# Inverse levels of the first mixer over all 16 heads, with the state chain of one token half between the levels of the other

## Chip, cores and metric

One core of one Trainium2 chip. The metric is the device time of one execution in microseconds (us), as the median of several runs. TensorE is called PE, VectorE DVE, ScalarE ACT, and the queue that issues all loads SP.

## What is computed

The reference runs two blocks over 256 tokens of width 2048, all in float32. The change is in the first mixer of the first block, an RWKV-7 recurrence over 16 heads of 64 channels. With a state S (64x64 per head) the reference steps token by token:

```
def step(state, inp):
    r_t, w_t, k_t, v_t, kk_t, a_t = inp
    sa = einsum('bhvk,bhk->bhv', state, -kk_t)
    state = state * w_t[:, :, None, :] + sa[..., None] * (kk_t * a_t)[:, :, None, :] + v_t[..., None] * k_t[:, :, None, :]
    return state, einsum('bhvk,bhk->bhv', state, r_t)
```

After it come a group norm over each head's 64 channels, a bonus term, a gate, and the product with `ev_w_out`. The other mixer, the feed-forward parts, the second layer and the whole second block are not touched.

## The kernel before

**The chunked form.** The kernel doesn't step over tokens. It cuts the 256 tokens into two halves of 128 (`tt` on PE and ACT, `th` on DVE) and these into four chunks `c` of 64. For every token half the work has these stages:

1. *Tokens* (`kbt`): 16 transposes bring the key-side operands BM and KM into token order (BTOK, KTOK).
2. *Pairs* (`g`): per head the products of BM and of KM (stationary, 64 rows x 128 columns) with AR (moving, 64 x 256: the "a" part and the "r" part side by side), lines 852 and 853. DVE multiplies each result by a causal mask into BF (one 128x256 tile per head) and KF.
3. *Values* (`gv`): KF times the value tokens, in two forms that alternate head by head: line 859 (stationary 128x128, moving 64 columns; result GVB) and line 860 (stationary 128x64, moving 128 columns; result YT). DVE copies both out.
4. *Inverse*: the inverse of (I - strictly lower triangular BF) by doubling, six levels `lv`. In a level DVE cuts a block pattern out of BF (TM, one mask operation per group of 4 heads); PE makes `u` = TM x M (line 875, 4 matmuls per group); ACT copies it to UU (line 1489); PE makes `m`, the updates of M and of its transpose (lines 886 and 887, 8 matmuls per group in two banks; in level 5 line 893, 4 matmuls in one bank); DVE adds them into MN (two operations per group). Level 0 has no `m`: DVE makes MN of `u` and of TM.
5. *State chain*, chunk after chunk: `x` (line 908, with the state ST), `sa` (line 918, the inverse applied; ACT copies it to SAQ, line 1498), `z` (927) and `y` (933) for the output, `s` (942, 943) for the new state, which DVE adds and scales (decay). `x` of the next chunk waits for that state.

When all is done, `group_norm_mean`, `group_norm_var` and eight DVE steps (`group_norm_step`: four reciprocals, four elementwise operations) of the token half follow. Those of half 0 are put between the work of half 1, those of half 1 stand alone at the end, before the product `ev_out` (lines 607, 612, 616).

**The order of the work.** Every engine runs a list written out by hand. All PSUM results of the mixer are "jobs": `mixer_jobs()` (line 109) gives each a number `j`; job `j` uses bank `j % 5`, PE opens it once job `j-5` is freed (`open_job`), and signals `mb_done` in the order of the numbers. Before the change stages 2 and 3 run over groups of 4 heads (`half`, `g`), and stage 4 over 8 heads at a time: two groups `g`, first for `half` 0 and then for `half` 1. So the PE order is tokens, (pairs, values) twice, six levels of 2 groups, (pairs, values) twice, six levels of 2 groups, chunk 0, chunk 1, and the same for the second token half with chunks 2 and 3. DVE does both `m` additions of both groups of a level and then both TM masks of the next level (lines 2001 to 2045).

**Buffers.** MN, TM, UU, KF and GVB lie in the arena `scr`, one set for two groups. The weights come through a ring of three slots of 2 MB (`ring`, `SLOT`). SP loads piece `n` when piece `n-3` is released (`piece_done`, line 195 on). The weights `bd` and `lora` of the mixer's elementwise part are in slots 1 and 2, are released as soon as their own products are done, and the three first pieces of `ev_out` are loaded over them in the shade of the mixer.

## Time and profile before

| | us |
|---|---|
| median of 3 runs | 3888.88 (3882.3 to 3890.7) |
| profiled execution, its own time | 3887.36 |
| its span in the trace | 3885.4 |
| mean granted PE clock over the span | 0.95 |
| PE busy | 3580.9 (92% of the span) |
| DVE busy | 2238.4 (58%) |
| ACT busy | 1694.9 (44%) |

The span is the time between the first and the last thing on the core; the profiled execution took 2.0 us more than that. The granted clock is 1.0 where PE runs at 2.4 GHz and 0.5 where it runs at 1.2 GHz; a stretch in between is a mix of both. A float32 matmul leaves two records on PE, so "x16" is eight matmuls.

### The profile page before, as it was taken

To read this page: it belongs to the slowest core of one execution; us is meant where nothing else is said; L and a number is where in the kernel's file an instruction comes from. 1 tells how busy PE (TensorE), PEld (TensorE's weight loads), DVE (VectorE), ACT (ScalarE), POOL (GpSimd) and SP (SyncE) were. 2 spreads that over 40 slices of the span, in tenths; PEclk is the share of its full clock that TensorE was granted. 3 is DMA by queue.
4 is the path that set the end of the run, shared out by engine and by line. 5 is a ranking of instruction groups with operands and counts; after the bars stand their busy time and mean duration, and the time that the engine had idled before them with its cause. 6 is when DMAs were issued, how large, how long until landed. Compare 5 with 4: busy or idle time off the path is not lost.

```text
span 3885.4 us, 56618 instructions
## 1 busy us (share of the span) xinstructions
PE 3580.9 (92%) x23084; PEld 3256.6 (84%) x23084; DVE 2238.4 (58%) x2732; ACT 1694.9 (44%) x2019; POOL 0.2 (0%) x4
## 2 busy tenths in 40 slices
PE   8985777889999899898898999989989999899988
PEld 7874666778888799897797888879989888898878
DVE  5566444556666644553545666664445667555674
ACT  4553110345565633342234655663334455444553
POOL 0000000000000000000000000000000000000000
PEclk9997877899999999999999999999999999999999
DMA  6440000335555345353143555534534443445332
GB/s 258 175 160 22 1 1 1 118 121 194 183 185 194 139 165 184 125 193 152 44 149 115 191 192 179 191 139 179 180 141 165 182 148 136 165 154 181 127 147 109
DMA packets 44788, 562.00 MB, mean 145 GB/s; under 512 B 4800, under 2 KB 6992, under 8 KB 7888
## 3 DMA queue, kind: packets, MB, share of 16 engines
q1 hardware_dynamic: 44624, 559.61, 39.7%
q8 instruction: 127, 2.08, 0.2%
q14 instruction: 37, 0.30, 0.0%
HBM read 557.47 MB, written 2.12 MB: 144 GB/s over the span
## 4 chain that ended last, share of the span: by engine, by line
PE 85%; DVE 8%; ACT 4%; issue 3%; DMA 0%; DVEq 0%; ACTq 0%; SPq 0%
PE bank L666 28%; PE bank L670 15%; PE bank L616 5%; PE bank L612 5%; PE bank L607 5%; PE bank L707 4%; PE bank L710 4%; PE bank L715 4%; PE bank L742 4%; DVE scr L1697 3%; PE bank L726 2%; PE bank L875 2%; ACT spl_r L1244 1%; PE bank L761 1%; PE bank L886 1%
## 5 line engine op out<-in xcount | busy, mean ns | idle before, releaser
L1697 DVE TENSOR_TENSOR spl_r<-ring,spl_r 128x2048 fp32r<-128x2048 f32 x416 | 952.5, 2291 | 656.9 <-ACT spl_r L1244 655.6
L666 PE MATMUL bank<-all_r,spl_r 128*128 128x512 f32 x5024 | 1214.4, 394 | 4.6 <-ACT spl_r L1244 4.6
L1244 ACT ACTIVATE spl_r<-ring 128x2048 fp32r<-128x2048 f32 x416 | 796.1, 1915 | 716.3 <-PE bank L670 391.5
L666 PEld LDWEIGHTS bank<-all_r,spl_r 128*128 128x128 f32 x5024 | 926.8, 188 | 195.1 <-ACT spl_r L1244 6.2
L670 PEld LDWEIGHTS bank<-all_r,spl_r 128*128 128x128 f32 x5120 | 656.7, 191 | 24.5
L670 PE MATMUL bank<-all_r,spl_r 128*128 128x256 f32 x5120 | 664.5, 283 | 0.0
L1697 DVE TENSOR_TENSOR dsp_r<-ring,dsp_r 128x1408 fp32r<-128x1408 f32 x128 | 207.4, 1625 | 288.7 <-ACT dsp_r L1244 288.7
L1244 ACT ACTIVATE dsp_r<-ring 128x1408 fp32r<-128x1408 f32 x128 | 176.0, 1380 | 295.3 <-PE bank L715 295.3
L1703 DVE SCALAR_TENSOR_TENSOR scr<-sumbuf,vec,scr 128x255 f32<-128x255 f32 (+2 forms) x379 | 182.1, 483 | 132.0 <-ACT scr L1337 80.7
L607 PE MATMUL bank<-scr_r,spl_r 128*128 128x256 f32 x1536 | 209.1, 289 | 37.1 <-ACT scr_r L1198 35.4
L607 PEld LDWEIGHTS bank<-scr_r,spl_r 128*128 128x128 f32 x1536 | 196.3, 195 | 41.4 <-ACT scr_r L1198 26.3
L707 PE MATMUL bank<-scr_r,dsp_r 128*128 128x256 f32 x1408 | 194.9, 288 | 26.0 <-ACT dsp_r L1244 22.9
L707 PEld LDWEIGHTS bank<-scr_r,dsp_r 128*128 128x128 f32 x1408 | 182.0, 196 | 27.6 <-ACT dsp_r L1244 24.3
L612 PE MATMUL bank<-scr_r,spl_r 128*128 128x256 f32 x1536 | 204.2, 287 | 0.0
L616 PE MATMUL bank<-scr_r,spl_r 128*128 128x256 f32 x1536 | 200.8, 284 | 1.4 <-DVE spl_r L1697 1.4
L612 PEld LDWEIGHTS bank<-scr_r,spl_r 128*128 128x128 f32 x1536 | 195.7, 196 | 0.0
L616 PEld LDWEIGHTS bank<-scr_r,spl_r 128*128 128x128 f32 x1536 | 192.1, 193 | 1.8 <-DVE spl_r L1697 1.8
L710 PE MATMUL bank<-lo_r,dsp_r 128*128 128x256 f32 x1408 | 192.9, 286 | 0.0
L715 PE MATMUL bank<-scr_r,dsp_r 128*128 128x256 f32 x1408 | 190.7, 284 | 0.0
L1337 ACT ACTIVATE scr<-sumbuf,vec 128x256 f32<-128x256 f32 x176 | 105.4, 599 | 188.3 <-DVE sumbuf L1697 188.2
L710 PEld LDWEIGHTS bank<-lo_r,dsp_r 128*128 128x128 f32 x1408 | 181.5, 195 | 0.0
L715 PEld LDWEIGHTS bank<-scr_r,dsp_r 128*128 128x128 f32 x1408 | 179.3, 193 | 0.0
(320 smaller groups left out, 3161.2 us busy)
## 6 DMA issues: line engine op xcount, KB each, us to landing
ring<-in_up SPq DMA_DIRECT2D x88, 2048.0 KB, 8.0
ring<-in_down SPq DMA_DIRECT2D x64, 1408.0 KB, 5.9
ring<-in_ib SPq DMA_DIRECT2D x34, 2048.0 KB, 8.0
ring<-in_ev_in SPq DMA_DIRECT2D x22, 2048.0 KB, 8.2
ring<-in_pg SPq DMA_DIRECT2D x16, 2048.0 KB, 8.1
ring<-in_out SPq DMA_DIRECT2D x16, 2048.0 KB, 7.9
ring<-in_in SPq DMA_DIRECT2D x12, 2048.0 KB, 7.9
ring<-in_ev_out SPq DMA_DIRECT2D x8, 2048.0 KB, 8.0
```

Source lines behind the costliest of these rows:

```text
L607: mm(out_, WHI[half][:, kk, :], rhi[:, kk, :], start=i_ == 0, stop=False)
L612: mm(out_, WHI[half][:, kk, :], rlo[:, kk, :], start=False, stop=False)
L616: one = mm(out_, WLO[half][:, kk, :], rhi[:, kk, :], start=False, stop=kk == DT - 1)
L666: mm(b[:, :], WHI[half][:, kk, :], pair(name, kk), start=kk == 0, stop=False, skip_group_check=True)
L670: one = mm(main, WLO[half][:, kk, :], rhi[:, kk, :], start=False, stop=kk == DT - 1, skip_group_check=True)
L707: mm(out_, DHI[half][:, kk, :], HHI[:, piece * FC + kk, :], start=first and kk == 0, stop=False, skip_group_check=True)
L710: mm(out_, DHI[half][:, kk, :], HLO[:, low_slot(piece * FC + kk), :], start=False, stop=False, skip_group_check=True)
L715: one = mm(out_, DLO[half][:, kk, :], HHI[:, piece * FC + kk, :], start=False, stop=last and kk == FC - 1, skip_group_check=True)
L742: one = mm(out, lhsT, rhs, start=n == 0, stop=n == len(terms) - 1)
L1244: A(high[half], w[:, :, half * P:(half + 1) * P], ACT.Copy).then_inc(S["w_hi"], 1)
L1697: return V.tensor_tensor(out, a, b, op)
L1703: return V.scalar_tensor_tensor(out=out, in0=a, scalar=s, in1=b, op0=op0, op1=op1)
```

## The change

- *Jobs and order* (`mixer_jobs` and the lists of PE, ACT and DVE): stages 2 and 3 run over `q`, 8 heads at a time, and stage 4 over four groups `g`, all 16 heads. A group is now 4 heads of one parity (`heads(g)`), so the two sides of a pair of matmuls write to two banks.
- *Pairs*: four kinds (BM or KM, with the "a" or the "r" part), each a matmul of 128 columns; the even and the odd head of a pair follow each other. BM and KM are so loaded as weights twice per head, not once. Kind 0 is copied out by ACT without a mask; kinds 1 to 3 are masked by DVE, 512 columns at a time.
- *Values*: eight matmuls of the one form (job `gb`), then eight of the other (`gy`). ACT copies both out.
- *Levels*: `u` for four groups, then `m` for four groups. DVE does per group two additions and, right behind them, the mask of the next level.
- *State chain*: chunks 0 and 1 don't follow the inverse of token half 0; they are put between the pairs and values of token half 1 and its levels 0 and 1. `x2`, the transposes `kbt1` and the group norm products of half 0 stand between its levels 1 to 4. `s` comes ahead of `z` and `y`. Only chunks 2 and 3 stay behind the inverse of half 1. The eight DVE steps of group norm 0 go from the levels of half 1 to these last chunks.
- *ACT at the end*: `rhs("ev_out", 0, 2)` moves to level 4 of half 1, and the first half of the first `ev_out` weight split ahead of chunk 2.
- *Buffers*: KF and MN of the four groups take ring slot 1 (the slot of `bd`), TM and UU slot 2 (that of `lora`), GVB goes to `xtra`, and BF is there once per token half. The pieces `bd` and `lora` are released by `nfin` 8, the end of the inverse of token half 1, and so the loads of `ev_out` pieces 1 and 2 wait for it.

```diff
--- before.py
+++ after.py
@@ -117,30 +117,31 @@
     add("lg", 4)
     add("vt", 4)
     add("bonus", 4)
+    add("kbt0", 4)
     for tt in range(2):
-        add(f"kbt{tt}", 4)
-        for half in range(2):
-            for g in range(2):
-                add(f"g{tt}{half}{g}", 4)
-                add(f"gv{tt}{half}{g}")
-                if tt and not half:
-
-                    add(("gnm0", "gnv0")[g], 2)
-            for lv in range(6):
-                for g in range(2):
-                    add(f"u{tt}{half}{g}{lv}")
-                if lv:
-                    for g in range(2):
-                        add(f"m{tt}{half}{g}{lv}", 2 if lv < 5 else 1)
-        for c in (2 * tt, 2 * tt + 1):
-            if c:
-                add(f"x{c}", 2)
-            add(f"sa{c}", 2)
-            if c:
-                add(f"z{c}")
-            add(f"y{c}")
-            if c < 3:
-                add(f"s{c}")
+        for q in range(2):
+            for kind in range(4):
+                for g in (2 * q, 2 * q + 1):
+                    order.append((f"g{tt}{g}", kind))
+            if tt:
+                add(("sa0", "x1")[q], 2)
+            add(f"gb{tt}{q}")
+            add(f"gy{tt}{q}")
+            if tt:
+                for key, n in ((("s0", 1), ("y0", 1)), (("sa1", 2),))[q]:
+                    add(key, n)
+        for lv in range(6):
+            for g in range(4):
+                add(f"u{tt}{lv}{g}")
+            if lv:
+                for g in range(4):
+                    add(f"m{tt}{lv}{g}", 2 if lv < 5 else 1)
+            if tt:
+                for key, n in ((("s1", 1), ("z1", 1), ("y1", 1)), (("x2", 2),), (("kbt1", 4), ("gnm0", 2)),
+                               (("gnv0", 2),), (), ())[lv]:
+                    add(key, n)
+    for key, n in (("sa2", 2), ("s2", 1), ("z2", 1), ("y2", 1), ("x3", 2), ("sa3", 2), ("z3", 1), ("y3", 1)):
+        add(key, n)
     add("gnm1", 2)
     add("gnv1", 2)
     norm("ln0")
...
-            last = {"bd": ("bd", 7), "lora": ("lg", 3), "uv": ("V", 15), "muq0": ("mq0", 2), "mukv0": ("mv0", 1),
+            if name in ("bd", "lora"):
+
+                piece_done.append(("nfin", 8))
+                g += n
+                continue
+            last = {"uv": ("V", 15), "muq0": ("mq0", 2), "mukv0": ("mv0", 1),
...
-        BF = scr[:, SPL:SPL + 4096].rearrange("p (u x) -> p u x", u=16)
-        KF = scr[:, SPL + 4096:SPL + 5120].rearrange("p (u x) -> p u x", u=4)
-        GVB = scr[:, SPL + 5120:SPL + 6144].rearrange("p (u x) -> p u x", u=16)
-        MN = [scr[:, a:a + 1024].rearrange("p (u x n) -> p u x n", u=4, x=2) for a in (SPL + 6144, 2048)]
-        TM = [scr[:, a:a + 512].rearrange("p (u x) -> p u x", u=4) for a in (SPL + 7168, 3072)]
-        UU = [scr[:, a:a + 512].rearrange("p (u x) -> p u x", u=4) for a in (SPL + 7680, 3584)]
+        BF = [scr[:, SPL + 4096 * t:SPL + 4096 * (t + 1)].rearrange("p (u x) -> p u x", u=16) for t in range(2)]
+        GVB = [xtra[:, 1024 * t:1024 * (t + 1)].rearrange("p (u x) -> p u x", u=16) for t in range(2)]
+        KF = [ring[:, SLOT + 1024 * g:SLOT + 1024 * (g + 1)].rearrange("p (u x) -> p u x", u=4) for g in range(4)]
+        MN = [ring[:, SLOT + 1024 * g:SLOT + 1024 * (g + 1)].rearrange("p (u x n) -> p u x n", u=4, x=2) for g in range(4)]
+        TM = [ring[:, 2 * SLOT + 512 * g:2 * SLOT + 512 * (g + 1)].rearrange("p (u x) -> p u x", u=4) for g in range(4)]
+
+        def heads(g):
+
+            return slice(8 * (g // 2) + g % 2, 8 * (g // 2) + 8, 2)
+
+        UU = [ring[:, 2 * SLOT + 2048 + 512 * g:2 * SLOT + 2048 + 512 * (g + 1)].rearrange("p (u x) -> p u x", u=4)
+              for g in range(4)]
...
+            def pairs(tt, q):
+
+                for kind, (left, which) in enumerate(((BM, 0), (BM, 1), (KM, 0), (KM, 1))):
+                    banks = [open_job((f"g{tt}{2 * q + side}", kind)) for side in range(2)]
+                    for x in range(4):
+                        a = 4 * q + x
+                        for side in range(2):
+                            rows = slice(64 * side, 64 * side + 64)
+                            one = mm(banks[side][:, x * P:(x + 1) * P], left[rows, a, tt * P:(tt + 1) * P],
+                                     AR[rows, a, tt, which, :], start=True, stop=True)
+                            if x == 3:
                                 done(one)

...
+            def values(tt, q):
...
+                for x in range(8):
+                    h = 8 * q + x
+                    one = mm(b[:, x * 64:(x + 1) * 64], KF[2 * q + h % 2][:, x // 2, 0:P], VTOK[:, tt, 64 * h:64 * h + 64],
+                             start=True, stop=True)
+                done(one)
+                b = open_job((f"gy{tt}{q}", 0))
...
+                    h = 8 * q + x
+                    rows = slice(64 * (h % 2), 64 * (h % 2) + 64)
+                    one = mm(b[rows, (x // 2) * P:(x // 2 + 1) * P], VTOK[:, tt, 64 * h:64 * h + 64],
+                             KF[2 * q + h % 2][:, x // 2, P:2 * P], start=True, stop=True)
+                done(one)
+
+            def level(tt, lv):
...
+                    pe.wait_ge(S["tm"], 24 * tt + 4 * lv + g + 1)
...
+                    b = open_job((f"u{tt}{lv}{g}", 0))
...
+                        rhs = MN[g][:, x, 0, :] if lv else m("ident")
+                        one = mm(b[:, x * P:(x + 1) * P], TM[g][:, x, :], rhs, start=True, stop=True)
+                    done(one)
+                for g in range(4):
+                    if not lv:
...
+            to_tokens(0)
+            for tt in range(2):
+                for q in range(2):
+                    pairs(tt, q)
+                    if tt:
+                        (solve, from_state)[q](q)
+                    values(tt, q)
+                    if tt:
+                        (outputs, solve)[q](q)
+                for lv in range(6):
+                    level(tt, lv)
+                    if tt and lv == 0:
+                        outputs(1)
+                    if tt and lv == 1:
+                        from_state(2)
+                    if tt and lv == 2:
+                        to_tokens(1)
+                        group_norm_mean(0)
+                    if tt and lv == 3:
+                        group_norm_var(0)
+            solve(2)
+            outputs(2)
+            from_state(3)
+            solve(3)
+            outputs(3)
             group_norm_mean(1)
             group_norm_var(1)
             product("ev_out")
...
             for tt in range(2):
...
+                        solve(0)
+                    values(tt, q)
+                    if tt and q == 1:
+                        solve(1)
+                for lv in range(1, 6):
+                    level(tt, lv)
+                    if tt and lv == 2:
+                        to_tokens(1)
+                        act.wait_ge(S["gn_c"], 1)
+                        A(AR[:, :, 0, 0, :], YT[:, 0:8, 0:P], ACT.Square).then_inc(S["gn_s"], 1)
+                    if tt and lv == 4:
+                        act.wait_ge(S["gn_e"], 1)
+                        A(AR[:, :, 0, 1, :], AR[:, :, 0, 1, :], ACT.Sqrt).then_inc(S["gn_q"], 1)
+                        rhs("ev_out", 0, 2)
+            split("ev_out", 0, 0, 1, (0,))
+            solve(2)
+            solve(3)
             group_norm(1)

             act.wait_ge(S["mb_done"], JOB[("gnv1", 1)] + 1)
...
+            def pairs(tt_, q):
+                for kind in (1, 2, 3):
+                    for g in (2 * q, 2 * q + 1):
+                        key = (f"g{tt_}{g}", kind)
+                        b = job_wait(key)
+                        dst = BF[tt_][:, heads(g), P:2 * P] if kind == 1 else KF[g][:, :, (kind - 2) * P:(kind - 1) * P]
+                        tt(dst, b[:, :].rearrange("p (u x) -> p u x", u=4),
+                           repeat(m("mask", 128, 0 if kind == 2 else 128), 4), ALU.mult).then_inc(job_free(JOB[key]), 1)
...
+                        for part in range(2):
+                            key = (f"m{tt_}{lv}{g}", part)
+                            b = job_wait(key)
+                            if part == 0:
+                                ve.wait_ge(S["mb_done"], JOB[(f"m{tt_}{lv}{g}", 1)] + 1)
+                            dst = MN[g][:, 2 * part:2 * part + 2, :, :].rearrange("p u x n -> p (u x n)")
+                            tt(dst, b[:, :], dst, ALU.add).then_inc(job_free(JOB[key]), 1)
+                        for part in range(2):
+                            key = (f"m{tt_}{lv}{g}", part)
+                            ve.wait_ge(job_free(JOB[key]), freed(JOB[key]))
+                        ve.engine_nop().then_inc(S["mn"], 1)
+                    else:
...
+                    if lv < 5:
+                        level_mask(tt_, lv + 1, g)
...
-                            V.tensor_copy(ST, src).then_inc(job_free(JOB[key]), 1)
-                        ve.wait_ge(job_free(JOB[key]), freed(JOB[key]))
-                        decay = pc[:, :].rearrange("p (a c) -> p a c", c=4)[:, :, c:c + 1].broadcast_to([P, 8, C])
-                        linked(tt(ST, ST, decay, ALU.mult), S["sq"], c + 1)
-                if th == 0:
-                    ve.engine_nop().then_inc(S["elem"], 1)
-
-                    link(tt(ZV, ZV, spread(v("gnb", 0, 8), 8), ALU.add))
+                for q in range(2):
+                    pairs(th, q)
+                    if th:
+                        (outputs, from_state)[q](q)
+                for g in range(4):
+                    ve.wait_ge(job_free(JOB[(f"g{th}{g}", 0)]), freed(JOB[(f"g{th}{g}", 0)]))
+                    level_mask(th, 0, g)
+                for lv in range(6):
+                    level(th, lv)
+                    if th and lv == 0:
+                        outputs(1)
+                    if th and lv == 1:
+                        from_state(2)
+                        link(tt(ZV, ZV, spread(v("gnb", 0, 8), 8), ALU.add))
+                    if th and lv == 2:
+                        group_norm_mean(0)
+                    if th and lv == 3:
+                        group_norm_var(0)
+            group_norm_step(0, 0)
+            group_norm_step(0, 1)
+            outputs(2)
+            group_norm_step(0, 2)
+            from_state(3)
+            for step in range(3, 6):
+                group_norm_step(0, step)
+            outputs(3)
             group_norm_mean(1)
...
```

## Rows read from the trace of the kernel before

**Rows 1.** The head of the page: span, and busy time of each engine.

```profile
span 3885.4 us, 56618 instructions
...
PE 3580.9 (92%) x23084; PEld 3256.6 (84%) x23084; DVE 2238.4 (58%) x2732; ACT 1694.9 (44%) x2019; POOL 0.2 (0%) x4
```

**Rows 2.** Busy time by stretch: us, then PE, PEld, DVE, ACT, POOL, clock, DMA share, GB/s.

```profile
352.00:371.84 19.84, 14.61 (x65) 9.95 (x64) 8.18 (x22) 0.71 (x2) 0.00 (x0) 0.66 0.00 1
371.84:418.20 46.36, 35.02 (x240) 33.87 (x240) 21.33 (x32) 5.97 (x10) 0.00 (x0) 0.85 0.00 1
418.20:437.96 19.76, 14.36 (x65) 9.93 (x64) 8.86 (x23) 0.00 (x0) 0.00 (x0) 0.71 0.00 0
437.96:486.70 48.74, 36.63 (x240) 35.38 (x240) 22.02 (x33) 5.98 (x10) 0.00 (x0) 0.80 0.00 1
486.70:514.20 27.50, 22.67 (x320) 21.93 (x320) 5.60 (x9) 2.37 (x4) 0.00 (x0) 0.53 0.01 2
514.20:542.70 28.50, 21.84 (x89) 13.80 (x88) 14.59 (x29) 5.33 (x7) 0.00 (x0) 0.74 0.00 0
542.70:588.30 45.60, 34.23 (x235) 33.28 (x236) 28.45 (x37) 6.33 (x11) 0.00 (x0) 0.85 0.00 1
588.30:608.90 20.60, 15.12 (x72) 10.49 (x70) 9.53 (x24) 0.00 (x0) 0.00 (x0) 0.72 0.00 1
608.90:656.70 47.80, 36.43 (x241) 35.25 (x241) 24.76 (x35) 5.98 (x10) 0.00 (x0) 0.80 0.00 1
656.70:683.87 27.17, 21.68 (x322) 20.74 (x321) 7.60 (x11) 2.37 (x4) 0.00 (x0) 0.60 0.00 1
683.87:712.79 28.92, 13.04 (x31) 7.54 (x32) 19.12 (x17) 9.61 (x8) 0.00 (x0) 0.50 0.00 1
```

**Rows 3.** Who waited for whom in 348.7 to 712.79, PE: total, times, longest.

```profile
PE bank L875 <- DVE scr L1697: 51.3, 24, 2.3
...
PE bank L859 <- DVE scr L1697: 16.9, 8, 2.8
```

**Rows 4.** Timeline of one level, 387.3 to 395.3: start, length, engine, line.

```profile
387.30 2.05 PE L875 MATMUL bank<-scr 128*128 128x128 f32 x16 [2.31 <-DVE scr L1697]
...
389.19 0.45 PE L886 MATMUL bank<-scr 128*128 128x128 f32 x2
...
391.30 1.42 DVE L1697 TENSOR_TENSOR scr<-bank,scr 128x512 f32<-128x512 f32 x2 [3.46 <-PE bank L887]
...
393.09 1.42 DVE L1697 TENSOR_TENSOR scr<-bank,scr 128x512 f32<-128x512 f32 x2 [0.37 <-PE bank L887]
...
394.55 1.29 DVE L1697 TENSOR_TENSOR scr<-scr,mat 128x512 f32<-128x512 f32 x2
...
395.29 3.18 PE L875 MATMUL bank<-scr 128*128 128x128 f32 x16 [2.31 <-DVE scr L1697]
```

**Rows 5.** Timeline of the first pairs and values, and half-speed values.

```profile
352.54 0.60 PE L853 MATMUL bank<-xb,scr 64*128 64x256 f32 x4
...
352.97 0.70 PE L852 MATMUL bank<-xb,scr 64*128 64x256 f32 x4
...
356.42 0.43 PE L859 MATMUL bank<-scr 128*128 128x64 f32 x2 [2.32 <-DVE scr L1697]
...
356.79 0.43 PE L860 MATMUL bank<-scr 128*64 128x128 f32 x2
...
365.37 0.69 PE L859 MATMUL bank<-scr 128*128 128x64 f32 x2 [1.47 <-DVE scr L1697]
```

**Rows 6.** Timeline of the state chain at half clock.

```profile
491.74 1.97 PE L933 MATMUL bank<-scr 64*64 64x64 f32 x32 [0.73 <-issue]
...
674.94 3.67 PE L918 MATMUL bank<-scr 64*64 64x64 f32 x32 [0.79 <-DVE scr L1697]
```

**Rows 7.** Timeline of the reciprocals of the last group norm.

```profile
696.10 5.33 DVE L1974 RECIPROCAL xb<-xb 128x256 f32<-128x256 f32 x3 [1.25 <-ACT xb L1474]
```

**Rows 8.** DMA issues of the page: KB each, us to landing.

```profile
ring<-in_ev_out SPq DMA_DIRECT2D x8, 2048.0 KB, 8.0
```

358 lines of the change are left out of this document (158 added, 200 removed).

## The prediction

> **What bounds the kernel now.** I read the head of the page first: PE is busy 92% of the span [rows 1], so over the whole kernel little is free. The table of stretches then shows that the mixer is another matter. From 352.0 to 683.87, the stretch that the change rewrites, 331.9 us pass, PE is busy about three quarters of each part, and its granted clock is 0.53 to 0.85 [rows 2]. What makes PE idle is the hand-over: in 24 places the first matmul of a level waits for DVE, 51.3 us in all, and in 8 places the values wait for DVE's masks, 16.9 us [rows 3]. The timeline of one level shows how. PE makes `u` in 387.30 to 389.19 (8 matmuls, 0.23 us each) and `m` until some 392.7 (16 matmuls); DVE starts its last two additions 0.37 us later, at 393.09, goes on to the masks at 394.55, and only then, at 395.29, PE may go on: a period of 8.0 us with 2.6 us of waiting at the full 2.4 GHz. The next level begins with 3.18 us for the `u` that took 2.05 us before: the clock had fallen to 1.2 GHz after the waiting [rows 4]. DVE and PE take turns because with two groups there is nothing else to do. With four there is.
>
> **The cost, part by part.** A full-speed matmul of 128x128x128 takes 0.223 us (5.4 us for the 24 of a level), a DVE operation on 512 columns 0.7 us [rows 4]. The ends of each range are in brackets.
>
> (a) *Pairs and values of half 0*, now 19.84 and 19.76 us [rows 2]. Pairs: two matmuls of 256 columns on the two row halves run together, one such pair per 0.43 us at full clock (352.54 to 352.97) [rows 5]. Eight heads are 16 pairs of 128 columns: 3.4 us, 6.9 at half clock. DVE's six masks take 4.2 and can begin half way, so they end about 2.9 or 1.5 us after PE. Values: now the two forms alternate, 0.37 us each (356.42 to 356.79) at full clock, and 0.69 instead of 0.43 at half [rows 5]. Eight of one kind in a row are unmeasured. Lower bound: the first form like a level's matmul, 0.223, the second two at a time as `y` is (16 of 64 columns in 1.97 us at half clock [rows 6]), together 2.7 us, 5.1 at half. Upper bound: nothing changes, 5.9 and 9.9. I take the lower one, since `y` has the same alternating output rows, and get 9.0 us per eight heads at full and 13.5 at half clock. This stretch runs at 0.66 to 0.71 now, so 12.5: 25 us for both [18 to 40].
>
> Each BM and KM is now loaded as weights twice, for 128 columns each time. In the level rows a load and a matmul of 128 columns take 0.223 us together [rows 4], against 0.215 us of streaming (half of the 0.43 in [rows 5]), so a load keeps up there and I add nothing. If the two sides' loads followed each other, 16 pairs would cost 32 x 0.223 = 7.1 us at full clock and 14.3 at half instead of 3.4 and 6.9, four times: 15 to 30 us more. This is the second rival below, and in the upper ends. The Trainium skill bears on it: by "TensorE: Matmul & The Clock Gate", part 2, on LDWEIGHTS, a load costs by its columns and not by its rows, so that a 64-row load is no cheaper than a full one.
>
> (b) *Inverse of half 0*, now 46.36 and 48.74 us [rows 2]. A level of four groups is 48 matmuls, 10.7 us. DVE needs per group 1.42 + 0.04 + 0.69 = 2.15 us and starts 2.2 us into `m` (8 matmuls, then 0.4 of hand-over), so its fourth mask is there 10.8 us after `m` began. PE fills 7.1 us with `m` and 2.7 with three `u`, waits 1.1, and makes the last: period 11.8 us, in place of 2 x 8.0 to 2 x 9.56. Levels 2 to 4: 35.4. Levels 0 and 1 are DVE's: 1.3 to its start, 4 x 2.05, a last `u`, then `m` 7.1 makes 17.5 us at full clock and 26.5 at half; I take 20, since the clock comes back within one level of full-size work in all four stretches (mean 0.80 to 0.85 [rows 2]). Level 5: 8.0. Sum 63 [57 to 72]. Banks do not stop it: the job five back is always one that ACT, or DVE a group earlier, has read. ACT's copies of `u` lie under the next group's `u`. ACT gets 2.4 us of copies per eight heads, and is busy only 6 of 46 us [rows 2].
>
> (c) *Chunks 0 and 1 and the front of half 1*, now 27.50 + 28.50 + 20.60 = 76.6 us [rows 2]. New front, PE at half clock: pairs 2 x 6.9, two solves 2 x 3.7 [rows 6], values 2 x 5.1, `x1` 3.7, `s0` 3.9 (32 matmuls at `y`'s pace), `y0` 2.0, together 41; at full clock 20.5. Such 64-row work holds the clock down (0.53 in 486.7 to 514.2 with PE busy 22.67 of 27.5 us [rows 2]), but the stretch is entered at full clock: 38 [24 to 52]. DVE has 14.6 us there (12 + 4 masks, 5 state operations) and stays below. Put into the levels: `s1`, `z1`, `y1` 7.9, of which 4.5 fill PE's wait for DVE in level 0; `x2` 2.5; tokens and group norm products 7.2 (the PE time of 514.2 to 542.7 less that of 352.0 to 371.84 [rows 2]). Together 13 [10 to 18].
>
> (d) *Inverse of half 1*, now 45.60 and 47.80 us [rows 2]: 63 as in (b) [57 to 72]. I add 5 for levels that begin at half clock behind chain work. Group norm 0's DVE mean and variance and the bias addition (some 5 us) lie in DVE's 3.2 us per level to spare and under tokens and the norm's products. Without that cover, 5 us.
>
> (e) *Chunks 2 and 3*, now 27.17 us [rows 2]. `x2` goes (3.3), and DVE's state update runs beside `y` since `s` comes first. The eight DVE steps come in: four reciprocals of 1.78 us [rows 7] and four of some 1.2, 12 us. They lie under the solves, `s2`, `z3`, `y3`, and the last two under ACT's square and the first variance product. Only the third delays `x3`'s addition, by 1.5. So 25.5 [22 to 28]; uncovered, they would cost 12.
>
> (f) *Nothing on the path*: the last group norm, 28.92 us [rows 2], where DVE sets the end and keeps its list; the ACT copies and the split moved ahead only fill idle ACT time. On SP, `ev_out` pieces 1 and 2 wait for the inverse of half 1, and all later loads queue behind them. They take 2 x 8.0 us [rows 8] and have (e) and (f), 54 us, before `ev_out` needs them. If that cover were gone, 16 us.
>
> **Sum.** Before 331.9 us. After 25 + 63 + 38 + 13 + 63 + 5 + 25.5 = 232.5. The gain is 99 us against the profiled execution's 3887.4 (1.5 below the median), so 3788 us.
>
> **Rivals.**
> - *Dips and queues take half of it.* Speaks for it: the upper ends, above all levels at a clock of 0.8 as now, with 48 matmuls at 0.28 us (13.4, 13 us more over eight levels), and chain work that pulls the levels behind it down. Against it: the dips now follow 2.3 us waits, and the new ones are 1.1 us or less. With all upper ends, 40 + 72 + 70 + 72 + 28 = 282 us: 3837.
> - *The weight loads bind in the pairs* (the price in (a)). For it: twice the loads. Against it: the level rows keep up. Then 3803 to 3818. The Trainium skill's rule on LDWEIGHTS, cited under (a), is on this side.
> - *PE stays at 1.2 GHz through the mixer: slower.* Place: the eight long levels, entered from 64-row stretches. The 480 inverse matmuls at 0.446 us are 214 us against 188.5 now; pairs and values 4 x 13.5 = 54; chunks 0 and 1, 22.7 [rows 2]; tokens and norm some 11; chunks 2 and 3, 27; twenty hand-overs of 0.5. Together 339, or 3895. It decides where the mean clock stays under 0.55. Against it: after each 64-row stretch now the inverse is back at a mean of 0.80 or more [rows 2].
> - *The change doesn't do what it says*: a wait in one list (ACT's copy of `sa` ahead of the values, DVE's `outputs(1)` ahead of level 1) keeps PE from running ahead, and the four groups go one after the other. Then a level takes what two levels do now and only the chunks gain, some 20 us: 3867.
>
> **How the numbers follow.** Forecast with its own range (3765 to 3815): 0.66. Weight loads bind: 0.10. Dips and queues: 0.12. Doesn't do what it says: 0.04. Half clock, slower: 0.03. Better than 3765, with the lower ends of (a), (c) and the levels: 0.05. The range 3765 to 3837 leaves out the last three, and a part of the third. A measurement of this kernel can tell about 0.2% (8 us) from no change. Faster by more: 0.95; within: 0.02; slower: 0.03.
>
> **What would show it.** In the profile after: the inverse stretches with a level every 11 to 12.5 us and PE busy over 90% of it, a clock near 1.0 from level 1 on; PE's wait for DVE in line 875's place down from 51 us to 15 or less, most of it in level 0; values of eight heads in 3 to 5 us; no wait of `ev_out` for a load; the last group norm still 28 to 30 us. It is wrong if the period of a level is over 13.5 us, if pairs take over 7 us at full clock, if the front of half 1 takes over 50 us, or if anything after the group norm moves by more than a few us.

## The result, and the profile after

The kernel after the change takes 3750.28 us (median of 4 runs, 3747.7 to 3751.76), against 3889.18 us before it (4 runs, 3882.3 to 3890.7, beside it on the same chip). The ratio is 0.9645, with a 95% interval of 0.9629 to 0.9662. The forecast was 3788, with a range of 3765 to 3837: the sign was right, the gain was 139 us and not 99, and the time lies below the whole range. The profiled execution after took 3747.7 us, the one before 3887.4.

The head of the page after answers to [rows 1]:

```profile
span 3745.9 us, 56805 instructions
...
PE 3504.6 (94%) x23212; PEld 3202.4 (85%) x23212; DVE 2219.0 (59%) x2674; ACT 1703.8 (45%) x2035; POOL 0.2 (0%) x4
```

PE executes 64 matmuls (128 records) more, since every product of the pairs is now two, and is busy 76 us less. Some 12 of these are the values, which no longer alternate (priced below); most of the rest is the same work at a higher clock. The table of stretches shows where. It answers to [rows 2], has the same columns, and its rows are the prediction's parts (a) to (f), with (c) and (d) cut where level 0 of half 1 begins:

```profile
352.26:374.16 21.90, 18.03 (x194) 16.62 (x193) 9.76 (x16) 4.56 (x8) 0.00 (x0) 0.81 0.01 1
374.16:433.93 59.77, 56.50 (x482) 55.05 (x482) 40.32 (x63) 12.54 (x21) 0.00 (x0) 0.99 0.00 1
433.93:456.91 22.98, 22.87 (x385) 21.70 (x385) 14.00 (x22) 6.34 (x11) 0.00 (x0) 1.00 0.01 2
456.91:524.30 67.39, 66.31 (x665) 62.87 (x664) 49.14 (x74) 21.36 (x31) 0.00 (x0) 1.00 0.01 1
524.30:547.18 22.88, 16.83 (x289) 16.13 (x289) 15.68 (x15) 2.37 (x4) 0.00 (x0) 0.69 0.48 185
547.18:575.86 28.68, 11.67 (x31) 6.97 (x32) 21.58 (x19) 5.92 (x5) 0.00 (x0) 0.56 0.00 1
```

Without the last row they sum to 194.9 us, where the prediction had 232.5 and the kernel before 331.9. The eye should go to the third and fourth rows. From 433.93 to 524.30 PE is busy 89.2 of 90.4 us and the granted clock is 1.0 (2.4 GHz), through the stretch of 64-row work that I had costed at half clock. The clock is low in the first, the fifth and the last row, where PE still waits.

The waits of PE in the stretch answer to [rows 3] (line 899 is the old 875, line 878 the old 859):

```profile
PE bank L878 <- DVE ring L1790: 3.9, 2, 1.9
PE bank L899 <- DVE ring L1790: 3.6, 8, 0.8
PE bank L947 <- DVE scr L1790: 2.7, 1, 2.7
```

The 51.3 us before the levels are 3.6 now, and the 16.9 us before the values are 3.9. The timeline of PE after shows the period of a level over 16 heads as the distance of two such rows, 11.29 us, where two levels of [rows 4] took 2 x 8.0 to 2 x 9.56:

```profile
395.31 1.16 PE L899 MATMUL bank<-ring 128*128 128x128 f32 x8 [0.31 <-DVE ring L1790]
...
406.60 1.16 PE L899 MATMUL bank<-ring 128*128 128x128 f32 x8 [0.31 <-DVE ring L1790]
```

The front of half 1 in PE's timeline (start, length) answers to [rows 5] and [rows 6]:

```profile
433.86 4.09 PE L865 MATMUL bank<-xb,scr 64*128 64x128 f32 x64
437.87 2.07 PE L947 MATMUL bank<-xtra,scr 64*64 64x64 f32 x32
439.88 2.00 PE L878 MATMUL bank<-scr,ring 128*128 128x64 f32 x16
441.81 1.09 PE L885 MATMUL bank<-ring,scr 128*64 128x128 f32 x16
```

Pairs of 8 heads take 4.0 us, a solve 2.07 (3.67 at half clock before) and the values of 8 heads 1.9 + 1.0 us, with no gap from one to the next.

### The profile page after: what moved, and what is told of

Read it like the earlier page. It is cut to its first block, busy times and chain, and to the rows that moved or that the text cites. A ratio compares the mean times of both kernels' runs of the same rounds, so it can differ in the third digit from the quotient of the medians.

```text
span 3745.9 us, 56805 instructions
## 1 busy us (share of the span) xinstructions
PE 3504.6 (94%) x23212; PEld 3202.4 (85%) x23212; DVE 2219.0 (59%) x2674; ACT 1703.8 (45%) x2035; POOL 0.2 (0%) x4
## 4 chain that ended last, share of the span: by engine, by line
PE 85%; DVE 8%; ACT 4%; issue 3%; DMA 0%; DVEq 0%; ACTq 0%; SPq 0%
PE bank L678 29%; PE bank L682 15%; PE bank L628 5%; PE bank L624 5%; PE bank L619 5%; PE bank L719 4%; PE bank L722 4%; PE bank L727 4%; PE bank L754 4%; PE bank L738 2%; DVE ring L1790 1%; DVE scr L1790 1%; ACT spl_r L1306 1%; PE bank L773 1%; DVE scr L1796 1%
## 5 line engine op out<-in xcount | busy, mean ns | idle before, releaser
L719 PEld LDWEIGHTS bank<-scr_r,dsp_r 128*128 128x128 f32 x1408 | 181.9, 196 | 27.5 <-ACT dsp_r L1306 24.2
```

Source lines behind the costliest of these rows:

```text
L719: mm(out_, DHI[half][:, kk, :], HHI[:, piece * FC + kk, :], start=first and kk == 0, stop=False, skip_group_check=True)
```

## The experiments

Two theories stood after the result. **A**: waiting of PE lowers its clock, so the gain is the waiting itself plus the half clock that followed it; the size of a matmul doesn't matter. **B**, the one on which the prediction's (c) rested: 64-row work by itself keeps the clock down. Beside that the parts of the change had to be priced: 16 heads in a level, masks made per group, the chain between the levels, the grouping of pairs and values. Every ratio below is against the kernel before, measured beside the run; its medians lay between 3886.4 and 3890.5 us. Numbers of us are differences of medians, if nothing else is said.

### Parts of the change undone

**Chain behind the inverse.** The chunks 0 and 1 are taken out of half 1 and run behind the inverse of half 0.

```
-                    if tt:
-                        (solve, from_state)[q](q)
...
+                if not tt:
+                    solve(0)
+                    outputs(0)
+                    from_state(1)
+                    solve(1)
+                    outputs(1)
```

> Chunks 0 and 1 of the state chain stand behind the inverse of token half 0 again, everything else is the changed kernel (3750 us). Theory A (the gain of the interleaving is the chain's waiting, and a clock that no longer falls): the chain stretch is back at some 25 to 27 us with a granted clock near 0.5 in its second half, the front of half 1 loses the chain's PE time at full clock (some 11 us) and starts at half clock, so 3750 + 15 to 22, about 3768 us. Rival B (the interleaving only moves work, PE time is what counts): within 5 us of 3750.

Measured: 3774.43 us (3769.48 to 3775.41), ratio 0.9706 [0.969, 0.9722], 24 us more than the change. PE's timeline of this kernel shows the waits that return (in brackets), and the second solve at half clock:

```profile
432.59 2.08 PE L945 MATMUL bank<-xtra,scr 64*64 64x64 f32 x32 [0.79 <-DVE scr L1787]
...
435.39 0.48 PE L963 MATMUL bank<-scr 64*64 64x64 f32 x4 [0.73 <-issue]
...
444.70 3.67 PE L945 MATMUL bank<-scr 64*64 64x64 f32 x32 [0.79 <-DVE scr L1787]
```

The clock falls around 435 and is 0.50 from 436 to 452. Waits of 0.8 us are much shorter than the 2.3 us of [rows 3]; the runs under "What stands between the pauses" come back to this.

**Levels over 8 heads.** Only the number of groups in a level goes back to two; masks stay per group.

```
-                for lv in range(6):
-                    level(tt, lv)
+                for step in range(12):
+                    level(tt, step % 6, 2 * (step // 6))
```

> The levels run over two groups (8 heads) at a time again, with the new buffers, pairs, values and interleaved chain. Theory A (DVE and PE take turns when there are two groups): a level of 8 heads takes 8.0 us at full clock against half of 11.3, for 16 such long levels 38 us more, with levels 0 and 5 some 46, so about 3796; with the dips of the clock as in the kernel before (9.56 us for some levels) up to 3812. Rival B (the gain came from the interleaved chain and the regrouped pairs and values): under 3770.

Measured: 3781.98 us (3779.51 to 3785.2), ratio 0.9726 [0.971, 0.9742], 32 us more than the change and less than expected. A level of 8 heads takes 7.26 us here, not the 8.0 to 9.56 of [rows 4]:

```profile
392.05 1.16 PE L900 MATMUL bank<-ring 128*128 128x128 f32 x8 [0.49 <-DVE ring L1792]
394.08 1.16 PE L900 MATMUL bank<-ring 128*128 128x128 f32 x8 [0.87 <-DVE ring L1792]
399.31 1.16 PE L900 MATMUL bank<-ring 128*128 128x128 f32 x8 [0.49 <-DVE ring L1792]
```

PE waits 26.7 us for DVE in all, in 34 pieces of at most 1.5 us, and the clock is 1.0 in these levels. So a part of what I had put down to the four groups belongs to the order of the masks; the run after the next one prices it.

**Masks last.** The change, but DVE makes the four masks of the next level behind the additions of all four groups.

```
-                    if lv < 5:
+                if lv < 5:
+                    for g in range(4):
```

> Four groups, but DVE makes the masks of the next level only after the additions of all four groups, as it did before for two. Theory A: the first matmul of a level waits for the last addition and one mask, 2.3 us or so after the last matmul; a level takes 13 to 13.5 us in place of 11.3, eight times, so 3765 to 3768. If waits of 2.3 us bring the clock down (Theory C: it is the waits that lower the clock), the levels go to 14 to 15 us in part of the cases and the time to 3775 to 3785; if only small matmuls lower it (rival D), the clock stays at 1.0 through the inverse of half 0.

Measured: 3766.94 us (3766.12 to 3767.3), ratio 0.9686 [0.967, 0.9702], 17 us more. PE's wait at line 899 is in 8 places again, but six of them are 2.28 us or longer. The first row has the columns of [rows 3]; the others, with the columns of [rows 2], show the clock behind the first two long waits:

```profile
PE bank L899 <- DVE ring L1790: 16.1, 8, 3.7
```

```profile
380.00:388.00 8.00, 5.62 (x26) 5.62 (x27) 3.97 (x7) 1.29 (x3) 0.00 (x0) 0.59 0.00 0
388.00:396.00 8.00, 8.00 (x72) 7.99 (x70) 3.87 (x6) 1.10 (x2) 0.00 (x0) 0.98 0.01 2
396.00:404.00 8.00, 5.72 (x37) 5.54 (x36) 3.79 (x6) 1.82 (x4) 0.00 (x0) 0.79 0.00 0
```

The same wait doesn't always do this. Behind the four other long ones the clock stays at 1.0, and the 16 `u` matmuls of a level take 3.84 us and not 5.47:

```profile
398.46 5.47 PE L899 MATMUL bank<-ring 128*128 128x128 f32 x32 [2.28 <-DVE ring L1790]
...
426.69 3.84 PE L899 MATMUL bank<-ring 128*128 128x128 f32 x32 [2.28 <-DVE ring L1790]
```

Where the clock holds, a level takes 13.26 us (426.69 to 439.95), as expected. The time too is the one that was expected without dips.

**Two groups and masks last.** Both of these together, the order inside a level that the kernel before has.

```
-                    if lv < 5:
+                if lv < 5:
+                    for g in range(first, first + 2):
                         level_mask(tt_, lv + 1, g)
```

> The kernel after the change with its levels over 8 heads (as in the run two_groups, 3782.0 us) and, on VectorE, the next level's masks made only after the additions of both groups, as the kernel before does it. Theory (the gain is the masks made per group, plus the idle time that this spares TensorE at the end of each level, idle time lowering the granted clock): a level of 8 heads takes 8.0 us at full clock in place of 7.26, 16 such levels give 11 us, and the longer waits (longest above 2 us) bring stretches of half clock, another 5 to 35 us: 3795 to 3830. Rival (the order of the masks is only worth its busy time, and the overlap of the two halves' work covers it): within 5 us of 3782.

Measured: 3807.89 us (3804.53 to 3813.68), ratio 0.9789 [0.9773, 0.9805], 26 us over the run with two groups alone. The level is 9.53 us long where the clock has fallen, and 7.96 where it holds (427.03 to 434.99):

```profile
388.34 3.38 PE L900 MATMUL bank<-ring 128*128 128x128 f32 x16 [2.28 <-DVE ring L1792]
397.87 2.75 PE L900 MATMUL bank<-ring 128*128 128x128 f32 x16 [2.28 <-DVE ring L1792]
```

**And the chain behind the inverse too.** The edits of the last run and of the first one together.

> The same as two_masks_last, and the chunks 0 and 1 of the chain run behind the inverse of half 0 instead of inside the one of half 1. The run chain_behind alone cost 24 us. If the parts add, this is 24 us over two_masks_last, some 3820 to 3855, and the clock shows 0.5 in the chain's stretch; what is left to 3889 is then the grouping of pairs and values and of the additions. Rival (the two share one cause, idle time of TensorE in the levels, so together they cost less than their sum): under 3815.

Measured: 3833.48 us (3825.58 to 3836.31), ratio 0.9856 [0.9839, 0.9872], another 26 us. Undone one on top of another, the parts are 32 us for two groups, 26 for the masks and 26 for the chain (24 when it was undone alone), and 57 us are left to the 3890.5 of the kernel before, for the grouping of pairs and values, `x2` and the tail. The price of a part depends on what it is undone with: the masks cost 17 us with four groups and 26 with two. Of these 57 the trace shows 17.6 in half 0: pairs and values of 16 heads take 22.0 us in this kernel (351.8 to 373.8) against 19.84 + 19.76 in [rows 2]. The other 39 us were not taken apart.

**Values in alternation.** The two forms of the values take turns, as before the change.

```
-                for x in range(8):
-                    h = 8 * q + x
+                    if x == 7:
+                        done(one)
```

> The two forms of the values' matmuls alternate again, instruction by instruction, now over 8 heads and with both banks open. Theory A (alternating between a full-width and a half-width stationary costs a drain each time): 0.37 us per matmul at full clock as before, 5.9 us per 8 heads in place of 3.0, four times, about 12 us more: 3762. Rival B (the forms cost the same in any order, the time went with the waits): within 3 us of 3750.

Measured: 3769.25 us (3764.44 to 3773.83), ratio 0.9701 [0.9686, 0.9716], 19 us more (22 by the ratios). Expected were 12 at full clock; here the clock also drops, to 0.50 from 364 to 372, where after the change it is 0.79 and then 1.00. At full clock, in half 1, this kernel shows a step of 0.37 us per matmul:

```profile
447.40 0.43 PE L879 MATMUL bank<-scr,ring 128*128 128x64 f32 x2
447.77 0.43 PE L884 MATMUL bank<-ring,scr 128*64 128x128 f32 x2
```

After the change 16 of them in two runs of eight take 2.9 us, 0.18 each. The Trainium skill ("TensorEngine Tiling (Array Packing)", Key Properties) says that a change of tiling mode drains the engine. The rows fit this, but none shows the drain itself.

**Sides one after the other.** The pairs take the four heads of one row half first and then those of the other.

```
-                    for x in range(4):
-                        a = 4 * q + x
-                        for side in range(2):
+                    for side in range(2):
+                        for x in range(4):
+                            a = 4 * q + x
```

> In the pairs the four matmuls of the even heads now come first and then the four of the odd heads, not in turn. Theory A (the two row halves work at the same time only when neighbours in the list use different halves): pairs of 8 heads go from 4.0 to 7 or 8 us at full clock, four times; part of it is hidden under DVE's masks, so 10 to 15 us more: 3760 to 3765. Rival B (PE reaches the other side's matmuls anyway, or the weight loads bind): within 3 us of 3750.

Measured: 3755.39 us (3748.86 to 3759.9), ratio 0.9659 [0.9644, 0.9673], 5 us more, inside the uncertainty, and less than the 10 to 15 expected. The timeline is clearer: pairs of 8 heads at full clock take 5.04 us here against 4.09, four times, which makes 4 us. So neither expectation holds, neither 7 to 8 us for the pairs nor no difference.

```profile
437.93 5.04 PE L865 MATMUL bank<-xb,scr 64*128 64x128 f32 x64
```

### What lowers the clock

**Small matmuls without a pause.** The change with 192 extra matmuls of 64x64x64 ahead of level 3 of half 1, and 384 on alternating row halves ahead of level 4; nothing uses them.

```
+                    if tt and g == 0 and lv in (3, 4):
+                        for n in range(192 * (lv - 2)):
+                            r = slice(0, 64) if lv == 3 or n % 2 == 0 else slice(64, 128)
+                            mm(b[r, 0:64], TM[0][r, 0, 0:64], MN[0][r, 0, 0, 0:64], start=True, stop=True)
```

> Extra matmuls without any wait stand in token half 1 ahead of level 3 (192 of 64x64x64 on one quarter of the array, one after the other) and ahead of level 4 (384 that alternate between two quarters). Their results are overwritten. Theory C (waiting lowers the clock, the size of the matmuls doesn't): the granted clock stays 1.0, the first block takes 21 to 24 us, the second 21 to 24, together 42 to 48 more than 3750. Rival D (64-row work lowers the clock): the clock falls to 0.5 inside the blocks, after which they run at half speed: 60 to 90 us more.

Measured in a single execution: 3798.37 us. The two blocks in the table of stretches:

```profile
492.97:515.51 22.54, 22.54 (x386) 22.47 (x385) 1.29 (x2) 1.06 (x1) 0.00 (x0) 1.00 0.01 2
...
528.14:550.69 22.55, 22.55 (x770) 22.48 (x769) 2.30 (x4) 0.00 (x0) 0.00 (x0) 1.00 0.01 4
```

For 22.5 us PE does nothing but 64-row work and the clock stays at 1.00. Theory B is out. (A side result: 384 matmuls on alternating row halves take the time of 192 on one.)

**Pauses of rising length.** DVE computes 1, 2, 3 and 5 extra reciprocals, whose results are not used, ahead of the first mask of levels 2 to 5, so that PE waits longer each time.

```
+                if g == 0 and lv >= 2:
+                    for _ in range((0, 0, 1, 2, 3, 5)[lv]):
+                        link(V.reciprocal(xtra[:, 8 * T:9 * T], VTOK[:, 0, 0:T]))
```

> DVE does 1, 2, 3 and 5 extra reciprocals (1.79 us each, results unused) ahead of the first mask of levels 2, 3, 4 and 5, in both token halves. PE so has waits of about 1.5, 3.3, 5 and 8.7 us in an otherwise unchanged run of full-size matmuls. Theory C (waits lower the clock): after the longer ones the next level begins at half clock, after the 1.5 us one not or seldom; 36 us of waiting and 6 to 15 us of half clock: 3792 to 3801. Rival D (only 64-row work lowers it): the clock is 1.0 in every level, 3785 or less.

Measured in a single execution: 3786.39 us, between the two times expected, so here the trace decides. Ahead of level 2 no wait is longer than 0.86 us. PE's timeline in half 0 shows the waits of levels 3 to 5 in brackets:

```profile
404.23 0.67 PE L910 MATMUL bank<-ring 128*128 128x128 f32 x2 [1.99 <-DVE ring L1790]
...
421.24 0.62 PE L910 MATMUL bank<-ring 128*128 128x128 f32 x2 [3.77 <-DVE ring L1790]
...
441.47 0.79 PE L910 MATMUL bank<-ring 128*128 128x128 f32 x2 [7.34 <-DVE ring L1790]
```

and the table of stretches shows the clock around the first of them (1.0 before, 0.57 behind, back at 1.0 in the next slice) and behind the last:

```profile
400.00:404.00 4.00, 2.24 (x21) 2.05 (x19) 3.93 (x4) 0.00 (x0) 0.00 (x0) 1.00 0.00 0
404.00:408.00 4.00, 3.77 (x19) 3.77 (x20) 3.37 (x7) 0.08 (x1) 0.00 (x0) 0.57 0.01 2
408.00:412.00 4.00, 3.63 (x33) 3.44 (x32) 1.87 (x3) 2.31 (x4) 0.00 (x0) 1.00 0.01 4
...
440.00:444.00 4.00, 2.53 (x12) 2.53 (x13) 3.83 (x7) 0.00 (x0) 0.00 (x0) 0.50 0.00 0
```

The fall comes behind the wait, in the work that follows it; the longest wait costs a few us of half clock like the shorter one, beside its own length. Together with the run with the masks last this says: a fall of the clock stands behind a wait, but not every wait of 2.3 us has one behind it.

### The same two causes in the kernel before

**Mask made early.** In the kernel before, DVE makes the next mask of a group right behind its additions and no longer ahead of the next level. The mask's own wait for `u` goes with it, since the additions have waited for more. Nothing else.

```
+                            if lv < 5:
+                                tt(TM[g], BF[:, h0:h0 + 4, 0:P], repeat(m("lmask", 128, 128 * (lv + 1)), 4), ALU.mult)\
+                                    .then_inc(S["tm"], 1)
```

> The kernel before, in which VectorE makes the mask of the next level for a group right behind that group's additions; nothing else. Theory: the period of a level over 8 heads falls from 8.0 to 9.56 us to some 7.3, the longest wait of TensorE there from 2.3 to under 1.6 us, and no stretch of half clock is left in the levels: 20 levels by 0.7 to 2.3 us, 14 to 45 less than 3889, so 3844 to 3875. Rival (the large gain needs all 16 heads in one level): 3880 or more.

Measured: 3847.77 us (3841.12 to 3851.28), ratio 0.989 [0.9873, 0.9906]: 43 us, nearly a third of the whole gain, from moving one operation. The period is 7.31 us (388.00, then 395.31):

```profile
388.00 1.16 PE L875 MATMUL bank<-scr 128*128 128x128 f32 x8 [0.52 <-DVE scr L1697]
...
395.31 1.16 PE L875 MATMUL bank<-scr 128*128 128x128 f32 x8 [0.52 <-DVE scr L1697]
```

**Filler.** In the kernel before, 8 extra matmuls of 128x128x128 ahead of each level's first wait; their results are not used.

```
+                            if lv and not g:
+                                for _ in range(8):
+                                    mm(b[:, 0:P], m("ident"), m("ident"), start=True, stop=True)
```

> The kernel before, with 8 extra matmuls of 128x128x128 on TensorE ahead of each level's first wait in the first mixer; their results are not used, nothing waits for them. If it is TensorE's waiting that lowers the clock in the levels, the levels of 9.56 us fall to some 8.0 and about 12 of 20 levels give 1.5 us each: 17 to 35 us less than 3889, so 3854 to 3872, with the granted clock at 1.0 in the levels. Rival (the clock has another cause, or the extra matmuls only delay the level): 3889 or up to 35 us more, with the clock as before.

Measured: 3861.42 us (3857.2 to 3864.28), ratio 0.9925 [0.9908, 0.9942]: more work and 29 us less. DVE's order is untouched, so the level can't be shorter than 8.0 us; it is 7.99 us every time. In the kernel before it is 9.56 us where the clock falls behind the wait (395.29 in [rows 4], then the first row here, then the second):

```profile
404.85 2.56 PE L875 MATMUL bank<-scr 128*128 128x128 f32 x16 [2.31 <-DVE scr L1697]
...
414.41 2.05 PE L875 MATMUL bank<-scr 128*128 128x128 f32 x16 [2.31 <-DVE scr L1697]
```

With the filler:

```profile
385.65 2.05 PE L878 MATMUL bank<-scr 128*128 128x128 f32 x16 [0.52 <-DVE scr L1700]
...
393.64 2.05 PE L878 MATMUL bank<-scr 128*128 128x128 f32 x16 [0.52 <-DVE scr L1700]
```

The rows from 376 to 416 have a clock of 1.0. This separates the two halves of a wait's price: its own length is still there (filled), and the half clock behind it is gone. The two runs fit each other: with the mask made early the period falls by another 0.68 us (7.99 to 7.31), for 20 levels an estimate of 14 us, and that run is 13.7 us faster than this one. So of its 43 us some 29 are the clock.

### What stands between the pauses

The run with the chain behind the inverse didn't fit theory A as it stood: its clock fell after waits of 0.79 and 0.73 us, while the levels of the run with two groups wait 0.49 and 0.87 us each time and keep 1.0. Two runs fill these waits of the chain, with 3 matmuls of 128x128x128 each or with 13 of 64x64x64; nothing uses them. The diff is the first one's.

```
+                b = open_job((f"sa{c}", 0))
+                fill(b, 3 if c < 2 else 0)
...
+                if c < 3:
+                    b = open_job((f"s{c}", 0))
+                    fill(b, 3 if c < 2 else 0)
```

> chain_behind (3774.4 us), with 3 extra 128x128x128 matmuls ahead of each of the four waits of chunks 0 and 1 (two solves, two updates of the state, each waits 0.73 to 0.79 us now); nothing uses their results. Theory (PE's waiting lowers the clock, also among 64-row work): the clock stays at 1.0 through the chain's stretch and the front of half 1, which at half clock cost some 15 to 20 us more than at full: 3754 to 3765. Rival (short waits as these don't matter, as they don't in the levels; 64-row work with any pause lowers it): the clock of 0.50 stays, 3774 or a little more.

> The same with 13 extra 64x64x64 matmuls (0.058 us each at full clock, 0.75 us in all) in the place of the 3 large ones. If waiting alone decides, as for the large ones: 3754 to 3765 and a clock of 1.0. If small matmuls hold the clock worse than large ones do, it falls here and not with the large ones: 3770 to 3776.

Measured: with large ones 3763.39 us (3761.03 to 3768.34), ratio 0.9685 [0.967, 0.97]; with small ones 3758.91 us (3756.12 to 3770.34), ratio 0.9667 [0.9652, 0.9682]. Filling the waits gives back 11 and 16 of the 24 us by the medians, 8 and 15 by the ratios; with large ones the interval still touches that of the unfilled run ([0.969, 0.9722]). With large ones the clock is 1.0 through the whole chain:

```profile
440.00:448.00 8.00, 7.42 (x137) 6.98 (x138) 2.63 (x4) 1.18 (x2) 0.00 (x0) 1.00 0.01 2
448.00:456.00 8.00, 6.51 (x139) 5.93 (x135) 5.87 (x10) 1.09 (x2) 0.00 (x0) 1.00 0.01 2
```

With small ones, in the profiled execution, it holds at 1.0 until 442 and falls after the one wait that is left, of 0.57 us. (With large ones the wait at this place is 0.58 us, and the clock stays at 1.0.)

```profile
440.00:448.00 8.00, 7.42 (x121) 7.29 (x118) 3.46 (x5) 0.00 (x0) 0.00 (x0) 0.68 0.01 2
448.00:456.00 8.00, 8.00 (x103) 8.00 (x104) 0.00 (x0) 1.18 (x2) 0.00 (x0) 0.50 0.00 0
```

That execution took 3770.34 us, the other three of the same kernel 3756.12 to 3760.29, so it fell in one execution and, by their times, not in the others. Filling the waits keeps the clock up, and every fall that was looked at in these traces stands behind a wait, that is shown. That small work around a short wait makes it more likely than large work does is suggested by this one profile and not settled.

### Better than both

**The tail.** The last group norm's factors are prepared earlier and its steps are split in halves, so that the split for the product, and its first matmuls, begin earlier.

```
+            link(tt(ZV[:, :, last], ZV[:, :, last], GG[:, :, last], ALU.mult))
+            link(tt(GG[:, :, last], GG[:, :, last], spread(v("gng", 0, 8), 8, P), ALU.mult))
...
+                tt(yv, yv, ZV[:, four, last], ALU.add).then_inc(S["mixed"], 1)
```

> A version meant to beat both kernels, at the end of the mixer only: the third DVE step of group norm 0 goes behind the addition that the last chunk waits for (1.7 us); the low parts of ev_out's right side for the second mixer and of its first weight half are made in DVE's idle time, and PE does their 24 matmuls ahead of the end of the group norm (3 to 4 us); the last gain and gate are folded into one factor ahead of time, and the last steps run by halves (1 to 2 us). Theory A (DVE's list sets the end of the mixer): 6 to 8 us less, 3743. Rival B (PE's own list was as late as DVE's there, at half clock): 2 to 3 us less, 3747.

Measured: 3747.74 us (3744.48 to 3748.29), ratio 0.9641 [0.9628, 0.9655]: 2.5 us less than the change, which a measurement can't tell from nothing. The first half unit of the product does end 5 us earlier in the trace (575.3 for 580.1), but half of it is not seen in the time. The 6 to 8 us expected were not reached.

**Fillers in what waits are left.** The tail of the last run, and extra matmuls ahead of the values of half 0, the solves of chunks 2 and 3 and one state update.

```
+                b = open_job((f"gb{tt}{q}", 0))
+                fill(b, 0 if tt else 8)
...
+                fill(b, (0, 0, 3, 11)[c])
```

> The kernel after with the tail of end_earlier (3747.7 us) and extra 128x128x128 matmuls in the places where PE still waits: 8 ahead of each values stage of half 0 (waits of 1.94 us), 3 ahead of solve and state update of chunk 2, 11 ahead of the solve of chunk 3 (a wait of 2.7 us). Theory: the clock stays at 1.0 from 352 to 547 and not at 0.57 to 0.8 in the first 24 us and 0.5 to 0.9 in the last 24; some 4 us less at the front and 2 to 4 at the tail: 3739 to 3744. Rival (the front is set by DVE's masks, the tail by its group norm, whatever PE's clock is): 3746 to 3749.

Measured: 3732.41 us (3731.55 to 3733.89, 5 runs), ratio 0.9603 [0.9589, 0.9616], against the change's 0.9645 [0.9629, 0.9662]: 16 us less by the ratios, and the intervals don't meet. This is more than the 6 to 8 expected. The first slices of half 0 in the table of stretches after the change:

```profile
356.00:360.00 4.00, 2.07 (x18) 1.90 (x15) 2.02 (x4) 0.00 (x0) 0.00 (x0) 0.85 0.02 4
360.00:364.00 4.00, 4.00 (x29) 3.55 (x30) 0.00 (x0) 1.19 (x2) 0.00 (x0) 0.50 0.00 0
```

and in this kernel:

```profile
356.00:360.00 4.00, 4.00 (x55) 3.76 (x56) 0.00 (x0) 1.43 (x3) 0.00 (x0) 1.00 0.00 0
360.00:364.00 4.00, 4.00 (x56) 3.84 (x53) 3.34 (x6) 0.85 (x2) 0.00 (x0) 1.00 0.02 4
```

From the first pair to PE's first wait in level 1 it is 22.95 us here (349.67 to 372.62) and 27.95 after the change (352.19 to 380.14). From the first pair to the end of the product's first half unit it is 218.5 us here (to 568.2) and 228.0 after the change (to 580.2). So 9.5 of the 16 us lie in the stretch, 5.0 of them ahead of the levels, where the first fillers are. The other 4.5 are the tail's edit and not fillers: from PE's first wait in level 1 to the end of the first half unit the run with the tail alone takes as long (195.5 us, 379.77 to 575.3) as this one (195.6), and the kernel after the change 200. The fillers of the chunks 2 and 3 keep the clock at 1.0 there and gain nothing, as the rival expected for the tail: DVE is busy 26.6 of the 28 us from 518 to 546. Another 2.6 us are there before the stretch begins (tokens start at 346.13 against 348.70), which no edit explains, and some 4 lie behind it; these I can't assign.

## Why the prediction was wrong in its size

**The step that failed** is the clock in (c) and (d): "Such 64-row work holds the clock down (0.53 in 486.7 to 514.2 with PE busy 22.67 of 27.5 us)", from which the front of half 1 was costed at 38 us and the inserts and dips in the levels at 13 + 5. Measured were 23.0 us and, for the inverse of half 1, 67.4 in place of 81: 15 + 13.6. Some 3 of the 13.6 are the difference of (b) over again; the inserts and dips cost 7.6 us (67.4 less the 59.8 of half 0) and not 18. So about 25 of the 37.6 us that the stages miss come from this step, though a part of the inserts is cheap because they fill waits that DVE leaves. I read a coincidence of small work and low clock as a cause, and this beside my own reading of [rows 4], where the clock had fallen behind a wait in full-size work. The rows held the other reading too: PE was idle 4.8 of those 27.5 us. The run with small matmuls in one unbroken block (clock 1.00 for 22.5 us) takes the cause away; the gaps, the filled levels of the kernel before and the filled chain give the other. Since the change removes the waits in this very stretch (22.87 busy of 22.98 us), it also removes the half clock.

- *(a) Pairs and values of half 0*: 21.9 us for 25. At full clock the values take 2.9 us per 8 heads, near the lower bound of 2.7 that I took; at half clock 5.1, as said. The pairs take 4.0, not 3.4: I had priced them at a pair's streaming time. The clock was 0.81 and not 0.66 to 0.71.
- *(b) Inverse of half 0*: 59.8 us for 63. The period is 11.29 for 11.8; PE's last wait is 0.31, not 1.1 us, since DVE starts 2.05 us into `m` and needs 2.03 us per group, where I had counted 2.2 and 2.15. The rest of the difference is in levels 0 and 1.
- *(c) and (d)*: above. The five us for dips were none, and tokens, norm products and chain cost in the levels what they take at full clock.
- *(e) Chunks 2 and 3*: 22.9 for 25.5. Here the dips are real: the clock is 0.69, and the solve of chunk 3 waits 2.7 us and then takes 3.67 us, as in [rows 6]. The run with fillers has it in 2.08, and the end of the mixer comes no sooner.
- *(f) Group norm*: 28.7 for 28.92. `ev_out`'s loads were issued at 525.05 and are over by 538, and nothing waited for them.
- Outside these stages 2.7 us are left: the stages fall by 331.9 - 194.9 = 137.0 us, and the profiled executions differ by 139.7.

**The rivals.** *Dips and queues* and *PE stays at 1.2 GHz* had the half clock right and its place wrong: it follows waits, and this change removes them. The Trainium skill ("TensorE: Matmul & The Clock Gate", on psum-queue depth-cycling) describes a clock that swings when PE idles briefly between groups of matmuls. The trace of the kernel before (a wait of 1.4 to 2.3 us in each level, clock 0.80 to 0.85 in the inverse) and the filler run (clock 1.0 in the levels) agree with it. *The weight loads bind in the pairs* was not so: it asked for 7.1 us at full clock and the pairs take 4.0, with their 64 load records in 3.90 us. The rule of the Trainium skill ("TensorE: Matmul & The Clock Gate", part 2) that a load costs by its columns is not enough to forecast this: with the sides one after the other the same load records take 4.84 us. That loads for the two row halves go on beside each other would explain both, but no run measured the loads alone. *Doesn't do what it says*: the lists ran as written.

**What I weighed wrongly beyond that.** I gave the masks no term of their own. The experiments price them: made early they are worth 26 us with levels of 8 heads, 17 with 16 heads, and 43 in the kernel before with nothing else changed. The four groups that give the change its name are worth 32 of the 139 when the masks are early already.

## What to carry to other kernels

A wait of the matmul engine costs its own length and can cost the half clock of what runs behind it, so look for both; before you regroup a pipeline, look whether the operation that releases the next round stands behind work that nobody waits for, as the masks did. Where a wait can't be removed, unused matmuls in it can pay (29 us in the kernel before; after the change 5 us that the trace shows ahead of the levels, and nothing in the chunks 2 and 3, where DVE's list sets the end). And before a low clock is put down to the kind of work in a stretch, look at the idle time inside and ahead of it.

## What the runs showed of the hardware

- Matmuls of 64x64x64 without a pause, 0.117 us each on one row half and 0.059 on alternating ones, keep the granted clock at 1.00 for 22.5 us.
- Waits of 0.49 and 0.87 us in each level of 7.26 us, among 128-row matmuls, left the clock at 1.0; waits of 1.99 and 2.28 us were followed by slices at 0.57 to 0.85 in some places, and by 1.0 behind four waits of 2.28 to 2.35 us in the run with the masks last. Among 64-row matmuls waits of 0.79 and 0.73 us, and in one execution a single one of 0.57, were followed by 0.50.
- In the run with rising pauses, half 0, the clock was back at 1.0 in the second slice of 4 us after 1.99 us of waiting, and one slice later after 3.77 and 7.34 us. In half 1 it took the later slice after 2.01 us too (0.78, 0.80, 1.00 from 508 to 520), so these runs don't tie the low stretch to the length of the wait.
- Matmuls that switch between a stationary of 128x128 and one of 128x64 with each instruction step by 0.37 us at full clock, and by 0.18 on average in two runs of eight.
- Pairs of 64-row matmuls are faster by a fifth (4.09 for 5.04 us per 32) when the row half changes with each matmul.
